# State-space heads of a two-block network: decay rows by one transfer per head, and the clamped differences shared by GpSimd and ScalarE

## What is computed

```
y[q] = sum_t  cb[t, q] * exp(-max(c[t] - c[q], 0)) * (x[t] * dt[t])      (t <= q forwards, t >= q backwards)
y    = (y + d_skip * x) * silu(z)
```

## Time and profile before

| | |
|---|---|
| runs, median of 3 | 2443.12 us (2442.75 to 2443.85) |
| profiled execution | 2443.01 us, its span 2441.1 us |
| TensorE busy | 2391.5 us, 98% |
| VectorE busy | 1713.4 us, 70% |
| ScalarE busy | 1339.5 us, 55% |
| GpSimd busy | 90.2 us, 4% |
| bytes read | 372.77 MB, 153 GB/s over the span |
| mean granted TensorE clock | 0.994 of full |

### The profile page before, as it was taken

The page is one execution under the profiler, slowest core; times in us unless marked ns, Lnnn a source line. Parts: engine busy times, 40 slices in busy tenths (PEclk is TensorE's granted clock), DMA queues, the critical chain, the costliest instruction groups (busy, mean ns, idle before and its releaser), DMA issues.

```text
span 2441.1 us, 48177 instructions
## 1 busy us (share of the span) xinstructions
PE 2391.5 (98%) x18842; PEld 2289.4 (94%) x18842; DVE 1713.4 (70%) x2517; ACT 1339.5 (55%) x2355; POOL 90.2 (4%) x101
## 2 busy tenths in 40 slices
PE   9999999999999999999999999999999999999998
PEld 8898999999899999999999997899999999789998
DVE  7788777777888867786766575676566657667665
ACT  6788655644678855563444445554444444555443
POOL 0000000000100000000100010010001001001000
PEclk9999999999999999999999999999999999999999
DMA  7454555455354455545455553345545544434553
GB/s 216 131 159 126 165 164 161 154 170 189 108 153 139 137 156 160 169 155 181 145 181 174 169 160 106 121 144 178 170 147 179 178 163 152 123 124 142 189 181 113
DMA packets 401046, 380.19 MB, mean 156 GB/s; under 512 B 28223, under 2 KB 397037, under 8 KB 400765
## 3 DMA queue, kind: packets, MB, share of 16 engines
q1 hardware_dynamic: 397821, 373.87, 48.0%
q10 hardware_dynamic: 3072, 4.20, 0.7%
HBM read 372.77 MB, written 1.05 MB: 153 GB/s over the span
## 4 chain that ended last, share of the span: by engine, by line
PE 79%; DVE 12%; ACT 3%; DVEq 3%; issue 1%; SPq 1%; DMA 1%; ACTq 0%
PE ps L583 22%; PE ps L585 21%; PE ps L584 21%; DVE scratch L1806 3%; DVE w_lo L1583 3%; DVEq L1805 2%; PE ps L805 2%; PE ps L836 1%; PE ps L837 1%; PE ps L838 1%; ACT scratch L1082 1%; ACT w_hi L1082 1%; PE ps L854 1%; PE ps L612 1%; PE ps L614 1%
## 5 line engine op out<-in xcount | busy, mean ns | idle before, releaser
L1583 DVE TENSOR_TENSOR w_lo<-raw,w_hi 128x1024 fp32r<-128x1024 f32 x664 | 812.0, 1229 | 423.2 <-ACT w_hi L1082 421.8
L583 PE MATMUL ps<-x_hi,w_hi 128*128 128x256 f32 (+1 forms) x3664 | 1056.4, 288 | 4.3 <-DVE w_lo L1583 1.6
L584 PE MATMUL ps<-x_lo,w_hi 128*128 128x256 f32 (+1 forms) x3664 | 1042.6, 285 | 0.0
L585 PE MATMUL ps<-x_hi,w_lo 128*128 128x256 f32 (+1 forms) x3664 | 1039.8, 284 | 0.0
L1082 ACT ACTIVATE w_hi<-raw 128x1024 fp32r<-128x1024 f32 x664 | 697.7, 1056 | 447.5 <-PE ps L585 370.6
L583 PEld LDWEIGHTS ps<-x_hi,w_hi 128*128 128x128 f32 x3664 | 690.8, 189 | 30.8 <-issue 25.3
L584 PEld LDWEIGHTS ps<-x_lo,w_hi 128*128 128x128 f32 x3664 | 692.2, 189 | 2.0
L585 PEld LDWEIGHTS ps<-x_hi,w_lo 128*128 128x128 f32 x3664 | 693.6, 189 | 0.0
L583 PE MATMUL ps<-big_r,w_hi 128*128 128x272 f32 (+1 forms) x832 | 238.9, 287 | 0.0
L585 PE MATMUL ps<-big_r,w_lo 128*128 128x272 f32 (+1 forms) x832 | 238.2, 286 | 0.0
L1082 ACT ACTIVATE scratch<-ps 128x256 f32<-128x256 f32 (+9 forms) x328 | 122.3, 384 | 154.9 <-PE ps L838 63.8
(11 more groups left out here) (302 smaller groups left out, 3063.1 us busy)
## 6 DMA issues: line engine op xcount, KB each, us to landing
raw<-in_w_in SPq DMA_DIRECT2D x184, 512.0 KB, 4.7
raw<-in_ffn_w_up SPq DMA_DIRECT2D x176, 512.0 KB, 4.3
raw<-in_ffn_w_down SPq DMA_DIRECT2D x64, 512.0 KB, 4.2
raw<-in_mix_w_in SPq DMA_DIRECT2D x64, 512.0 KB, 4.6
scratch<-in_w_in SPq DMA_DIRECT2D x40, 512.0 KB, 4.8
raw<-in_w_mem_kv SPq DMA_DIRECT2D x32, 512.0 KB, 4.8
raw<-in_w_br_ssd SPq DMA_DIRECT2D x32, 512.0 KB, 3.8
raw<-in_ffn_w_down SPq DMA_DIRECT2D x32, 384.0 KB, 3.3
```

What stands on the lines that cost most here:

```text
L583: mm(out, wh, xh, start=first, stop=False)
L584: mm(out, wh, xl, start=False, stop=False)
L585: return mm(out, wl, xh, start=False, stop=last)
L1583: tt(w_lo[:, p % PARTS, :, :], raw_at(slot_of(Q, p))[:, :, (p % 2) * P:(p % 2 + 1) * P], wh_f[:, p % PARTS, :, :], ALU.subtract).then_inc( ...
```

## The change

Rows now come by transfer. ScalarE copies the 32 rows, negated, in fp32, to `cum_rows` and at once sends the table (64 KB) to a DRAM buffer. Heads 0 and 1 of a layer are still spread by TensorE, with plain fp32 operands (a broadcast identity column by the 32x512 table). For each of the other 30 heads of a layer ScalarE issues a transfer that reads the head's 2 KB row into all 128 partitions (256 KB) of `even_row` or `odd_row`; it does so behind the decays of head h-2. The two wide pieces of a head's clamped difference are computed by GpSimd from that row (add the token's c, then max with 0), the two narrow ones by ScalarE. For the first two heads of groups 1 to 3 the results go into a buffer of their own in `gates`, so that GpSimd can make them ahead. The square additions of GpSimd are put between heads. `head_sel`, the row remainder of VectorE and the clearing by GpSimd are gone. On VectorE the remainders of tiles 11 and 12 are made behind the weighing of heads 0 and 1, every remainder of the loop is one tile later, and that of tile 19 stands behind the last gating. GpSimd's loop over layers is written out.

```diff
-        cum_rows = nc.alloc_sbuf_tensor_at("cum_rows", [P, 2 * SEQ], F32R, offset=big_at + 4 * 7168)
+        cum_rows = nc.alloc_sbuf_tensor_at("cum_rows", [P, 2 * SEQ], F32, offset=big_at + 4 * 7168)
+        even_row = nc.alloc_sbuf_tensor_at("even_row", [P, 2 * SEQ], F32, offset=big_at + 4 * 7680)
...
-        head_sel = sb("head_sel", [P, SSD_HEADS], F32R)
+        odd_row = sb("odd_row", [P, 2 * SEQ])
+        rows_dram = nc.dram_tensor("cum_rows_dram", (DEPTH, SSD_HEADS, 2 * SEQ), F32, kind="Internal").ap()
...
         expo = view(scratch, 0, 2, 768)
+        first_expo = view(gates, 4608, 2, 768)
+        cuts = ((0, 0, slice(0, 256), slice(0, 256)), (0, 1, slice(256, 384), slice(128, 256)),
+                (1, 0, slice(384, 512), slice(256, 384)), (1, 1, slice(512, 768), slice(256, 512)))
...
+        head_row_in = [sem("even_head_row_in"), sem("odd_head_row_in")]
...
                  "o_var o_rsq att_ready dg_tanh cg_tanh cs_done cs_max cp_ready cn_ready "
...
             pool.drain()
             pool.sem_inc(S["skip_ready"], 1)
-            with pool.Fori(0, DEPTH) as l:
+            def add_square(l, n):
                 pool.drain()
-                pool.memset(cum_rows[2 * SSD_HEADS:P, :].bitcast(F32), 0.0).then_inc(S["rows_cleared"], 1)
+                pool.wait_ge(S["y_squared"], l * 16 + n + 1)
+                pool.tensor_tensor(y_sum[:, :], y_sum[:, :], y_sq[:, n % 2, :], ALU.add).then_inc(S["sq_added"], 1)
+
+            for l in range(DEPTH):
                 pool.drain()
                 pool.memset(y_sum[:, :], 0.0)
-                with pool.Fori(0, 4 * GROUPS // 2) as p:
-                    for t in range(2):
-                        pool.drain()
-                        pool.wait_ge(S["y_squared"], l * 16 + p * 2 + t + 1)
-                        pool.tensor_tensor(y_sum[:, :], y_sum[:, :], y_sq[:, t, :], ALU.add).then_inc(S["sq_added"], 1)
+                pool.wait_ge(S["cum_ready"], l + 1)
+                for h in range(2, SSD_HEADS):
+                    g, j = h // HEADS_PER_GROUP, h % HEADS_PER_GROUP
+                    pool.wait_ge(head_row_in[h % 2], 16 * (l * 15 + h // 2))
+                    pool.wait_ge(S["decay_ready"], l * SSD_HEADS + h - 1)
+                    for d, t, to, of in (cuts[0], cuts[3]):
+                        at = d * SSD_HEADS + h
+                        m = pool.tensor_scalar((first_expo if j < 2 else expo)[:, h % 2, to], (even_row, odd_row)[h % 2][:, of],
+                                               cum_tok[:, t, at:at + 1], 0.0, ALU.add, ALU.max)
+                    m.then_inc(S["expo_ready"], 1)
+                    if j == 6:
+                        add_square(l, 4 * g)
+                    if j == 1:
+                        for n in range(1, 4):
+                            add_square(l, 4 * (g - 1) + n)
+                for n in range(1, 4):
+                    add_square(l, 4 * (GROUPS - 1) + n)
                 add_bias(l, SEQ)
             with pool.Fori(0, 3 * DEPTH - 2) as n:
                 add_bias(n + DEPTH, TOK2)
...
                         for k in range(9, 9 + 1):
                             proj(Q, T, k, k, x1)
                         cumulate()
+                        pe.wait_ge(S["row_ready"], l + 1)
                         pe.wait_ge(S["cum_ready"], l + 1)
-                        pe.wait_ge(S["row_ready"], l + 1)
-                        pe.wait_ge(S["rows_cleared"], l + 1)
-
-                    def spread_rows(j):
-                        if j >= 2:
-                            pe.wait_ge(S["expo_ready"], G * 8 + j - 1)
-                        h = g * HEADS_PER_GROUP + j
-                        sel = head_sel[:, h:h + 1].to_broadcast([P, P])
-                        mm(ps[2 + j % 2][:, :], sel, cum_rows[:, :], start=True, stop=True).then_inc(S["bc_done"], 1)
+                        for h in range(2):
+                            mm(ps[2 + h][:, :], const[0:SSD_HEADS, K_ID + h:K_ID + h + 1].to_broadcast([SSD_HEADS, P]), cum_rows[0:SSD_HEADS, :],
+                               start=True, stop=True).then_inc(S["first_rows"], 1)
                     def head_pair(p):
                         if p >= 2:
...
                                 if n == 3:
                                     m.then_inc(S["y_done"], 1)
-                    spread_rows(0)
-                    spread_rows(1)
                     for j in range(HEADS_PER_GROUP):
                         if j < 7 and (g or j >= 1):
                             proj(Q, T, 9 + j, 9 + j, x1)
-                        if j + 2 < HEADS_PER_GROUP:
-                            spread_rows(j + 2)
                         if j % 2 == 1:
                             head_pair(j // 2)
...
             def small_params():
                 act.wait_ge(params_in, 16 * 4)
                 fn(neg_a[:, :, :], neg_a[:, :, :], ACT.Exp).then_inc(S["nega_exp"], 1)
-                copy(head_sel[2 * SSD_HEADS:P, :], const[2 * SSD_HEADS:P, K_ID:K_ID + SSD_HEADS])
-                for r in (0, SSD_HEADS):
-                    m = copy(head_sel[r:r + SSD_HEADS, :], const[r:r + SSD_HEADS, K_ID + r:K_ID + r + SSD_HEADS])
-                m.then_inc(S["sel_ready"], 1)
                 act.wait_ge(S["lam_dot"], 1)
                 fn(stats[:, 4:8], stats[:, 0:4], ACT.Exp).then_inc(S["lam_exp"], 1)
...
                             act.wait_ge(S["dt_pre"], l + 1)
                             fn(dt_x[:, 2, :], dt_x[:, 1, :], ACT.Exp).then_inc(S["dt_exp"], 1)
+                    def fetch_row(h):
+
+                        act.wait_ge(rows_out_done, 16 * (l + 1))
+                        if h >= 4:
+                            act.wait_ge(S["relu_done"], l * 30 + h - 3)
+                            act.wait_ge(S["expo_ready"], l * 30 + h - 3)
+                        act.dma_start((even_row, odd_row)[h % 2][:, :], rows_dram[l, h].unsqueeze(0).to_broadcast([P, 2 * SEQ])).then_inc(head_row_in[h % 2], 16)
+
                     def z_tile(j):
                         done(T, 6 + j)
...
                         z_tile(3)
                     if g == 0:
                         act.wait_ge(S["row_done"], l + 1)
-                        copy(cum_rows[0:SSD_HEADS, :], ps[3][0:SSD_HEADS, :]).then_inc(S["row_hi"], 1)
+                        copy(cum_rows[0:SSD_HEADS, :], ps[3][0:SSD_HEADS, :], -1.0).then_inc(S["row_ready"], 1)
+                        act.wait_ge(S["row_ready"], l + 1)
+                        act.dma_start(rows_dram[l], cum_rows[0:SSD_HEADS, :]).then_inc(rows_out_done, 16)
                         copy(cum_tok[:, :, :].rearrange("p t h -> p (t h)"), ps[2][:, 0:2 * 64]).then_inc(S["cum_ready"], 1)
                         act.drain()
-                    cuts = ((0, 0, slice(0, 256), slice(0, 256)), (0, 1, slice(256, 384), slice(128, 256)),
-                            (1, 0, slice(384, 512), slice(256, 384)), (1, 1, slice(512, 768), slice(256, 512)))
-
                     def decays(j):
-                        act.wait_ge(S["bc_done"], G * 8 + j + 1)
-                        for d, t, to, of in cuts:
-                            at = d * SSD_HEADS + g * HEADS_PER_GROUP + j
-                            m = fn(expo[:, j % 2, to], ps[2 + j % 2][:, of], ACT.Relu, scale=-1.0, bias=cum_tok[:, t, at:at + 1])
-                        m.then_inc(S["expo_ready"], 1)
+                        h = g * HEADS_PER_GROUP + j
+                        e = (first_expo if g and j < 2 else expo)[:, j % 2, :]
+                        if h < 2:
+                            act.wait_ge(S["first_rows"], 2 * l + j + 1)
+                            for d, t, to, of in cuts:
+                                fn(e[:, to], ps[2 + j][:, of], ACT.Relu, bias=cum_tok[:, t, d * SSD_HEADS + h:d * SSD_HEADS + h + 1])
+                        else:
+                            act.wait_ge(head_row_in[j % 2], 16 * (G * 4 + j // 2 - l))
+                            for d, t, to, of in cuts[1:3]:
+                                m = fn(e[:, to], (even_row, odd_row)[j % 2][:, of], ACT.Relu, bias=cum_tok[:, t, d * SSD_HEADS + h:d * SSD_HEADS + h + 1])
+                            m.then_inc(S["relu_done"], 1)
+                            act.wait_ge(S["expo_ready"], l * 30 + h - 1)
                         act.drain()
                         if j >= 4:
                             act.wait_ge(S["y_done"], G * 8 + j - 3)
-                        fn(decay[:, j % 4, :], expo[:, j % 2, :], ACT.Exp, scale=-1.0).then_inc(S["decay_ready"], 1)
+                        fn(decay[:, j % 4, :], e, ACT.Exp, scale=-1.0).then_inc(S["decay_ready"], 1)
+                        if g * HEADS_PER_GROUP + j + 2 < SSD_HEADS:
+                            fetch_row(g * HEADS_PER_GROUP + j + 2)
                     def gate(j):
                         done(T, 10 + j)
...
                     if g == 0:
                         dt_softplus()
                     split(Q, 10)
-                    split(Q, 11)
-                    split(Q, 12)
```

(14 more changed lines are left out.)

5 lines of the change are left out of this document (3 added, 2 removed).

## The result

| | before | after |
|---|---|---|
| median of the runs, us | 2442.93 (2440.95 to 2443.85) | 2483.93 (2480.51 to 2485.15) |
| span of the profiled execution, us | 2441.1 | 2483.3 |
| start of GpSimd's norm bias addition at the end of layer 0 and of layer 1, us | 617.85, 1209.90 | 639.42, 1251.02 |

The ratio is 1.0167 [1.0154, 1.0179]: the change makes the kernel slower by 41.0 us. The forecast was 2432 us with a range of 2416 to 2468, so both the direction and the range were wrong.

What follows compares the result with a forecast made beforehand. TensorE, busy 98%, was taken to bound, in a chain also through VectorE. Period 57.45 to 55.8 us: six groups at 1.6 and two first groups at 0.9 take 11.4 us off 2443.0, giving 2432 us, range 2416 to 2468.

Steps and rivals of the forecast that it cites:

- row loop: Head stage: a row is fetched only when head h-2 is clamped, so two heads cost L + P + 0.2, 5.9 us.
- P: Time of a head's two wide GpSimd operations in the row loop: between 0.6 and 3.4 us, taken as 2.2.
- L: Time from issue to landing of a 256 KB row transfer: between 2.3 and 4.7 us, taken as 3.5.
- rival C: Row loop too slow with L = 4.7 and P = 3: about 3.9 us more a group, 2474 us; chance 8%.
- TensorE: State-space groups: 64 row spreads go, 1.84 us a group; its own work per period becomes 54.33 us.
- The moved remainders: VectorE, before the heads: two remainders go behind the first weighings; first pair ready 2.27 us earlier, its 1.11 us wait gone.
- ScalarE: Head stage: 0.7 us saved on each of 60 heads, 42 us; issuing 62 transfers beside the exponential costs nothing.
- Exclusion, rival B: From first to last weighing, VectorE and GpSimd keep each other out: period 60.5, 3.0 us more, 2467 us; chance 22%.
- First groups: First group of each layer: the table's DRAM trip adds some 2.5 us before head 2; 0.9 us saved each overall.
- Rival A: State-space groups: TensorE alone decides, L + P under 5.5, period 54.33, 3.1 us saved a group, 2420 us; chance 15%.
- Rival D: State-space groups: nothing is left, holds of 3 instead of 1.5 us give the gain back, 2443 us; chance 14%.
- the third segment: From a group's last head pair to the next group's first convolution tap: shrinks only from 7.06 to about 6 us.

Runs made afterwards that it cites:

- the floor: Changed kernel with four row buffers and GpSimd's operations on 16 columns of both wide pieces, the other 240 left out: 2424.26 us, 0.9923 of the kernel before.

## Why the prediction was wrong

**The step that failed** is the size of both terms of the row loop, first of all P, by the price of GpSimd's wide operation: 0.5 us, put between the memset (0.32) and the two-operand addition (0.74) because "one wide operation reads one SBUF operand". The upper bound was no bound. The form costs 1.14 us alone; in its place 1.70 on average, since it also stands behind VectorE (shown under *Exclusion* below). P came out at 3.39, not 2.2, and at the very end of the 0.6 to 3.4 that was given for it. Its own work is 2.28 of that and the waits 1.1; the forecast had 1.0 and so 1.2. So the waits were right and the operation was not. L is the second: the 3.5 us are right as the median of all fetches, but the rows of heads 5, 6 and 7, on which the loop turns, have a median of 5.1, above the upper bound of 4.7.

**From there by the prediction's own sum.** With P alone put right L + P is 6.9, where 5.7 was taken: three stages of 1.2 more a group, less the 0.5 that fits and the 1.6 gained, lose 1.5 us a group, about 2455 us. (By the same terms the loop makes the kernel slower than before from L + P = 6.4, not from the 7.2 that the prediction names.) The other 29 us lie in what the sum lacked. A turn of the loop takes 8.8 and 8.3 us and not 6.0, since the rows of the middle heads land late and since head 7 stands behind head 6 and a square addition. The first two rows land together, and head 3 stands behind head 2 on GpSimd, so the first stages pay P twice (131.45 to 138.53). And the clock falls, see below. The last exponential was put 22.6 us after ScalarE's start of heads, and TensorE was to want it weighed at 24.6; it ended at 156.6, 30.4 after 126.21. It is *rival C's* mechanism, the row loop, at 8% and 2474 us, with a P and an L (3 and 4.7) close to those of the middle heads. That P and L both count is shown: taking the columns out of P returns 48.2 us, the landing out of the loop 36.8, both 59.7.

**A price nobody had: the clock.** In six of the eight groups TensorE waits 3.4 to 3.8 us before the last pair, and its granted clock is 0.50 for two microseconds and more after it (rows above), so its next products run at 1.2 GHz. The period from 95.38 to 157.73 is 8.43 us over the floor's 53.92; the pairs' waits are 5.96 of that, and one wait for a gate's tanh 0.49. That leaves 2.0, and the clock accounts for 1.7: its mean is 0.57 over the 4 us from 96 to 100. The prediction named a clock that falls as a sign of being wrong, but gave it no price.

**TensorE**: right, a little low. 54.33 us was forecast as its own period; 53.92 was measured, and with eight spreads at 0.23 that is 55.76, the period of the kernel with only the remainders moved.

**The moved remainders**: right. The 1.11 us wait before the first pair goes, no other comes, and alone they give 10 us. They were more than half of what was good in the change: with the loop out of the way the spreads that are gone add 1.84 a group to that.

**ScalarE**: the saving (40 us) and the free issue beside the exponential (0.33 us) were right. That ScalarE needs relief at all, once the spreads are gone, the prediction did not say; the run with four clamps on it shows it for two row buffers. Four buffers with all four clamps on ScalarE were not run.

**Exclusion, rival B (22%)**: false here. VectorE's remainders have a mean of 1246 and 1278 ns in the changed kernel from 120 to 240 us, against 1220, and its weighings 973 against 954:

```profile
L1608 DVE TENSOR_TENSOR w_lo<-raw,w_hi 128x1024 fp32r<-128x1024 f32 x21 | 26.1, 1246 | 0.0
L1871 DVE TENSOR_TENSOR big<-big,scratch 128x768 f32<-128x768 f32 x16 | 15.4, 973 | 19.1 <-ACT big L1092 19.0
```

With some 15 remainders and 8 weighings a group that is under 1 us a group, of the 5.6 forecast. The two engines do keep each other out, but GpSimd pays. A remainder runs from 133.12 to 134.33 us: it starts inside a GpSimd operation and still takes 1.21, while the GpSimd operation that starts inside it, at 133.57, takes 1.77 and ends 1.01 after it. The Trainium skill ("SBUF — State Buffer", Who interferes with whom) has whoever issues first hold the shared ports for its whole instruction and the other block. The trace agrees for GpSimd behind VectorE and not the other way round: VectorE loses 26 to 58 ns a remainder on average, and GpSimd's operation grows from 1.14 to 1.70 us.

**First groups**: forecast 0.9 us saved each, measured 4.75 lost in layer 0 and, without the 2.4 of the attention blocks in between, 5.7 in layer 1. The rows can't be there before the table's trip through DRAM, and the row loop follows. The two plain fp32 spreads, put at 0.9 us a layer, take 1.95 in layer 0 (62.50 to 64.45) and 3.06 in layer 1.

**Rival A (2420 us, 15%)** was right on what TensorE could do if nothing else stood in the way: the floor version has 2424.3, with 3.5 us given back in the attention blocks.

**Rival D and the hidden wait for the additions**: the prediction saw that the third segment would hardly shrink; the run with the squares earlier shows that this costs nothing as long as the row loop sets the pace.

## What to carry over

Price an operation by a row of the same form on the same engine; a form with fewer operands is not a lower bound on anything, and where no row has the form, the range must reach well past the nearest ones. A fetch that may start only when its buffer is consumed puts the landing and the consumer's work in one loop, so deepen the buffer before handing that work to a slower engine: here four buffers and half of the hand-over gave 17 us where two buffers and all of it cost 41. A median landing time hides the fetches that matter: read it for the stretch in which the loop turns. Taking work off the engine that bounds is worth something only as far as every engine behind it can arrive earlier too, and the engine that gives up the work should give up no more than is needed.

## What the runs showed of the hardware

- GpSimd, 128x256 fp32: scalar form with two operations 1.14 us, with one constant 0.85, two operands 0.61, copy 0.41, memset 0.31; the first on 128 columns 0.72, on 16 columns 0.34. VectorE takes 0.348 for the first.
- The same GpSimd operation has a mean of 1.70 us in the changed kernel and of 2.28 in the one with four buffers and one piece, where VectorE is busy 51.89 of 57.5 us instead of 43.87. There most of it is hidden.
- A 2 KB row of DRAM read into all 128 partitions (256 KB) lands in 3.0 to 6.7 us in the changed kernel. By buffer the medians are 3.4 and 3.7 there, and up to 4.9 in other versions.
- An activation with a column bias and an input from SBUF took ScalarE 506 and 398 ns (256 and 128 columns), from PSUM 477 and 369.
